# Inner tiles of six feed-forward stages in parts of 8, 8 and 6 instead of 8, 6 and 8, and where small work stands at their end

## The chip, the cores and the metric

The program runs on one core of one Trainium2 chip. The metric is device time: microseconds of the one core from start to end of a launch. The kernel before took 3107.2 us, the median of 3 runs (3106.8 to 3108.93).

## The reference

Input is x, 512 tokens of 1024 features, in float32. Twelve stages follow each other, each a residual around a normalized input. Two layers of the first block are: feed-forward, a mixer, feed-forward. Two layers of the second block are: a mixer (in layer 0 with rotary positions, in layer 1 a linear recurrence with decays), cross-attention to a memory, feed-forward. So six of the stages are feed-forward, and all six have the same form (cut to it):

```
D_MODEL = 1024; SEQ = 512; D_FF = 2816; D_FF_2 = -(-8 * D_MODEL // (3 * 256)) * 256   # = 2816

def _swiglu(x, w_gate, w_up, w_down):
    return (jax.nn.silu(x @ w_gate) * (x @ w_up)) @ w_down

x = x + MACARON * _swiglu(_rmsnorm(x, ffn1_norm), ffn1_w_gate, ffn1_w_up, ffn1_w_down)   # first block, MACARON = 0.5
x = x + swiglu(rms_norm(x, ffn_norm[layer]), ffn_w_gate_up[layer], ffn_w_down[layer])    # second block

def rope_tables(positions):          # needed by the first mixer of the second block
    inv_freq = ROPE_BASE ** (-jnp.arange(0, QK_ROPE_DIM, 2, dtype=jnp.float32) / QK_ROPE_DIM)
    ang = positions.astype(jnp.float32)[..., None] * inv_freq
    return jnp.cos(ang), jnp.sin(ang)
```

## The kernel before, in words

Everything lies with features on the 128 partitions and the 512 tokens along the row: x is 8 tiles of 128 x 512, the 2816 inner features of a feed-forward are KF = 22 inner tiles, and its output is 8 output tiles, called m = 0 to 7. The six feed-forward stages are f = 0 to 5 in the code and **FFN 0 to 5** in this text. In the list of the twelve stages (i = 0 to 11) they stand at F_STAGE = (0, 2, 3, 5, 8, 11). FFN 0 and 2 are followed by the first block's mixers, FFN 1 directly by FFN 2, FFN 3 (i = 5) by the mixer with rotary positions (M2_STAGE, i = 6), FFN 4 (i = 8) by the mixer with decays (M3_STAGE, i = 9), and FFN 5 is the end.

**Precision.** Each product is taken in three: the operands are split into a high part and a low part (high x high, high x low, low x high). Weights arrive in units of 128 x 1024 float32 in one stream, by DMAs that SP issues (line 3238) into slots; ScalarE makes the high part (`split_hi`, line 1218, tile whi), GpSimd the low part (`lo`, line 3121, wlo). Of the normalized input, ScalarE makes the high slice gxh (line 1273) and VectorE the low slice gxl (line 2161). SP loads into a slot again once the unit in it has been split.

**Parts.** The inner tiles go in three parts, `F_PARTS`: tiles 0 to 7, 8 to 13, 14 to 21. For each part the kernel computes gate and up of its tiles and then multiplies by the weights of `down`. The first two parts are taken in blocks: a product of 2 x 2 blocks is made from seven products of blocks (the steps `seven(s)`), on 256 columns, in lines 640, 641 and 644. There is a step for each inner tile (gate and up) and, for each of the first two parts, four `down` steps of two output tiles each. A product of a `down` step has 3 matmuls for each pair of inner tiles: 12 in the first part's, 9 in the second part's. The sums of blocks that the seven products need are made by VectorE (lines 2207 to 2225); some of the additions of their results are GpSimd's (`part`, line 3157), and the last ones into x are VectorE's (`c22`, line 2238, and `first_row`, line 2259; for an inner tile they go into a bank, lines 2233 and 2255). TensorE's fourth product of the next step (`fourth(s - 1)`, written for the step before it) waits for c22's result.

**The last part** is classical, on 512 columns, in lines 501 to 505: eight units, m = 0 to 7, of as many pairs of high and low inner tiles as the part has, 3 matmuls each. The first X_EARLY = 3 units are held open in three banks: first all their pairs but the last two, then the fourth product of the last inner tile, then the last two pairs of each (the "rests"). Units 3 to 7 follow whole. In FFN 5 the last unit is taken in two halves of 256 columns (`last_tile`).

**An inner tile** m passes from TensorE to VectorE's gate (line 2272), ScalarE's silu, GpSimd's scaling (`scale`, line 3129, tile f_s), VectorE's hidden product (line 2286, tile f_u), and then its high part (`hidden_hi`, ScalarE, line 1314) and its low part (`hidden_lo`, GpSimd, line 3134). These go into halves of tiles f_oddh/l, f_tur0h/l (function `hidden_tile`). Tiles of the first two parts are also turned into blocks by VectorE and ScalarE. PAIRED is the first tile of the last part.

**The residual** comes after each stage, in rounds m = 0 to 7: VectorE adds unit m's bank to x (line 2150), ScalarE makes gxh and the squares, VectorE the slice gxl (line 2161) and the sum of squares (line 2168). The next stage's first matmuls read the slices in order, the last one (m = 7) at last. When the next stage is a feed-forward, the rounds also turn the slices into blocks (`turn_parts`, `turn_lo`). The residual after FFN 3 has a second sum of squares (line 2177), and the 12 operations of `rope_angles` (lines 2021 to 2039) stand ahead of round 1 and a sign multiplication (line 2140) ahead of round 4, after ScalarE's two sines. The residual after FFN 4 has `decay_bounds` ahead of round 1, `decay_rates` ahead of 3 and `reset_positions` ahead of 4.

**Order.** Each engine's program is written out by hand in the order in which it runs; semaphores are its only waits. An instruction waits behind all that stands ahead of it on its engine. GpSimd's order at the end of an FFN is in `ffn` at line 3160 and on, VectorE's in `step(s)`.

Of the kernel before, what the change touches and what calls it, by code (L numbers as in the profile page):

```python
# [13 lines left out]
P = 128  # L14
# [43 lines left out]
F_PARTS = ((0, 8), (8, 14), (14, 22))  # L58
F_RUNS = ((0, 9), (9, 15), (15, 22))
# [116 lines left out]
def freed(u):  # L176

    if u in SEVEN:
# [9 lines left out]
          for m in range(X_EARLY + 1, KD if i == F_STAGE[5] else KD + 2)}  # L188

# [54 lines left out]
class Memory:  # L244
# [72 lines left out]
    def mixer2_tiles(self):  # L317
        outer = self.stack
        with ExitStack() as st:
# [9 lines left out]
                ("rcos", SEQ, F32), ("rsin", SEQ, F32), ("inv", 4 * 16, F32),  # L329
# [58 lines left out]
def hidden_tile(M, T, m):  # L388

    if m >= PAIRED:  # L390
        k = m - PAIRED
        name, k = ("odd", (k + 3) % 4) if k < 4 else ("tur0", k - 4)
        return seq(T[name + "h"], k), seq(T[name + "l"], k)
# [68 lines left out]
def tensor_program(pe, S, M):  # L462
# [132 lines left out]
    def last_tile(pairs):  # L595
# [4 lines left out]
        for half in range(2):  # L600
            b = next_bank("xs", 11, KD - 1, half)
            for k in range(KD):
# [5 lines left out]
            for k in range(KD):  # L608
                mm = pe.matmul(b[:, 0:HALF], seq(lo, k, P), of_half(pairs[k][0], half), start=False, stop=k == KD - 1)
# [8 lines left out]
    def ffn(f):  # L618
# [589 lines left out]
def scalar_program(act, S, M, T_in):  # L1208
    bank = M.bank

    def split_hi(u):
# [6 lines left out]
        act.activation(M.whi[r][:, :], M.raw[r][:, :], ACT.Copy).then_inc(*S.tick("hi", u))  # L1218
# [23 lines left out]
    def residual(i, keys):  # L1242
# [58 lines left out]
    def ffn(f):  # L1301
# [64 lines left out]
        def step(s):  # L1366
# [629 lines left out]
def vector_program(dve, S, M):  # L1996
# [124 lines left out]
    def residual(i, last, scale):  # L2121
# [75 lines left out]
    def ffn(f):  # L2197
# [114 lines left out]
        def step(s):  # L2312
# [781 lines left out]
def pool_program(pool, S, M):  # L3094
# [13 lines left out]
    def lo(u):  # L3108
# [6 lines left out]
        if u in SEVEN and SEVEN[u][0] == 2:  # L3115
# [5 lines left out]
        pool.tensor_tensor(M.wlo[r][:, :], M.raw[r][:, :], M.whi[r][:, :].bitcast(F32), ALU.subtract).then_inc(  # L3121
            *S.tick("lo", u))

    def ffn(f):
# [52 lines left out]
        for s, item in enumerate(SEQS[f]):  # L3177
# [19 lines left out]
            if before[0] == "tile":  # L3197
# [225 lines left out]
```

## Time and profile before

| | |
|---|---|
| median of 3 runs | 3107.2 us (3106.8 to 3108.93) |
| the profiled execution's own time | 3106.85 us |
| span of its trace | 3105.6 us |
| TensorE, matmuls (PE) | 3080.5 us busy, 99% |
| TensorE, weight loads (PEld) | 2827.1 us, 91% |
| VectorE (DVE) | 2168.9 us, 70% |
| ScalarE (ACT) | 1624.8 us, 52% |
| GpSimd (POOL) | 1650.7 us, 53% |
| matmuls | 20424 |
| DMA | 322.61 MB, mean 104 GB/s |

All is one execution, seen from its span's start, in microseconds. PE's busy time covers matmuls that overlap each other (a matmul's own duration is longer than the distance to the next one's start), so the pace of the stream is read from the starts. "x" with a number is a count of instructions. A timeline row has the start, the duration, the engine, the line of the kernel, the operation, output and inputs, and in brackets the idle time ahead of it with what ended it.

### The profile page before, as it was taken

The numbers are of one execution on the slowest core, as the hardware profiler recorded it, in microseconds if no ns is written. First come the engines' busy times: TensorE is split into PE (matmuls) and PEld (weight loads), VectorE is DVE, ScalarE is ACT, GpSimd is POOL, SyncE is SP. The second block draws the span as 40 slices with busy tenths as digits, with TensorE's granted clock in tenths as the row PEclk, the third lists the DMA queues.
The fourth block names the chain that finished last, engine by engine and source line by source line (L and its number), as shares of the span: only waits on it lengthen the run. The fifth ranks groups of instructions, "written<-read, shape, count | busy, mean of one in ns | idle before, by whom it ended". The sixth has DMA issues, their size and how long they took to land. (4 is left out here: it accounts for less than half of the span.)

```text
span 3105.6 us, 52754 instructions
## 1 busy us (share of the span) xinstructions
PE 3080.5 (99%) x20424; PEld 2827.1 (91%) x20424; DVE 2168.9 (70%) x2975; ACT 1624.8 (52%) x2567; POOL 1650.7 (53%) x994
## 2 busy tenths in 40 slices
PE   9999999999999999999999999999999999999999
PEld 8999888999989998888999877889999788889998
DVE  8776467877668774577877578558775786478773
ACT  6555433555556554335555455556554575455553
POOL 5676433677657675434767433226676112257674
PEclk9999999999999999999999999999999999999999
DMA  4323322232322232322223232322232223323232
GB/s 141 113 103 123 120 76 75 102 110 109 123 86 105 109 117 102 113 82 82 109 107 112 93 95 82 118 93 106 99 122 105 95 93 121 114 89 109 109 110 82
DMA packets 93320, 322.61 MB, mean 104 GB/s; under 512 B 10512, under 2 KB 14992, under 8 KB 93072
## 3 DMA queue, kind: packets, MB, share of 16 engines
q1 hardware_dynamic: 87680, 312.07, 28.5%
q10 hardware_dynamic: 5392, 7.17, 0.7%
q8 instruction: 164, 2.69, 0.4%
q14 instruction: 84, 0.69, 0.1%
HBM read 316.05 MB, written 2.10 MB: 102 GB/s over the span
## 5 line engine op out<-in xcount | busy, mean ns | idle before, releaser
L3121 POOL TENSOR_TENSOR wlo<-raws,whi 128x1024 fp32r<-128x1024 f32 x369 | 891.8, 2420 | 1135.8 <-ACT whi L1218 884.4
L1218 ACT ACTIVATE whi<-raws 128x1024 fp32r<-128x1024 f32 x422 | 441.0, 1051 | 159.2 <-PE bank L505 57.2
L3129 POOL TENSOR_TENSOR f_s<-f_s,R 128x512 f32<-128x512 f32 x132 | 172.4, 1306 | 193.8 <-ACT f_s L1308 192.4
L640 PE MATMUL bank<-gxh,whi 128*128 128x256 f32 x1064 | 268.8, 283 | 1.2 <-ACT acc L1364 1.2
L641 PE MATMUL bank<-gxl,whi 128*128 128x256 f32 x1064 | 268.6, 283 | 0.0
L2219 DVE TENSOR_TENSOR wlo<-banks,whi 128x1024 fp32r<-128x1024 f32 (+1 forms) x166 | 196.9, 1186 | 68.9 <-ACT whi L1335 68.9
L640 PE MATMUL bank<-f_th,f_sh 128*128 128x256 f32 x944 | 236.9, 283 | 0.0
L641 PE MATMUL bank<-f_tl,whi 128*128 128x256 f32 x944 | 236.7, 283 | 0.0
L640 PE MATMUL bank<-f_th,whi 128*128 128x256 f32 x944 | 236.7, 283 | 0.0
L641 PE MATMUL bank<-f_tl,f_sh 128*128 128x256 f32 x944 | 236.7, 283 | 0.0
L501 PE MATMUL bank<-gxh,whi 128*128 128x512 f32 x584 | 229.9, 394 | 1.4 <-DVE gxl L2161 1.4
L1335 ACT ACTIVATE whi<-banks 128x1024 fp32r<-128x1024 f32 (+1 forms) x166 | 165.2, 995 | 122.6 <-DVE banks L2212 122.2
L1364 ACT ACTIVATE sq<-bank 128x256 f32<-128x256 f32 x332 | 125.8, 379 | 194.9 <-PE bank L644 193.3
L502 PE MATMUL bank<-gxl,whi 128*128 128x512 f32 x584 | 227.4, 389 | 0.0
L3118 POOL TENSOR_TENSOR f_sl<-raws,f_sh 128x512 fp32r<-128x512 f32 x166 | 217.0, 1307 | 13.1 <-ACT f_sh L1349 13.1
L2207 DVE TENSOR_TENSOR banks<-raws 128x1024 f32<-128x1024 f32 (+1 forms) x166 | 210.0, 1265 | 0.0
L640 PEld LDWEIGHTS bank<-gxh,whi 128*128 128x128 f32 x1064 | 204.2, 192 | 1.8 <-ACT acc L1364 1.6
L641 PEld LDWEIGHTS bank<-gxl,whi 128*128 128x128 f32 x1064 | 204.2, 192 | 0.2
L2225 DVE TENSOR_TENSOR f_sl<-banks,f_sh 128x1024 fp32r<-128x1024 f32 (+1 forms) x166 | 195.3, 1176 | 0.0
L2286 DVE TENSOR_TENSOR f_u<-bank,f_s 128x512 f32<-128x512 f32 x132 | 91.3, 691 | 145.4 <-DVE f_sl L2225 83.7
L640 PEld LDWEIGHTS bank<-f_th,f_sh 128*128 128x128 f32 x944 | 181.2, 192 | 0.5 <-issue 0.2
L641 PEld LDWEIGHTS bank<-f_tl,f_sh 128*128 128x128 f32 x944 | 181.2, 192 | 0.2
(597 smaller groups left out, 9192.7 us busy)
## 6 DMA issues: line engine op xcount, KB each, us to landing
raws<-stream SPq DMA_DIRECT2D x588, 512.0 KB, 3.3
xa_mem<-memT ACTq DMA_DIRECT2D x2, 1024.0 KB, 6.2
m_dk<-decay ACTq DMA_DIRECT2D x2, 514.0 KB, 4.5
x<-xT ACTq DMA_DIRECT2D x4, 256.0 KB, 5.3
x<-xT SPq DMA_DIRECT2D x4, 256.0 KB, 6.6
outT<-x SPq DMA_DIRECT2D x2, 512.0 KB, 3.0
m_ct<-cos ACTq DMA_DIRECT2D x2, 256.0 KB, 2.6
m_sn<-sin ACTq DMA_DIRECT2D x2, 256.0 KB, 2.9
```

Source lines behind the costliest of these rows:

```text
L501: pe.matmul(out, seq(hi, k, P), h, start=first and k == 0, stop=False)
L502: pe.matmul(out, seq(hi, k, P), l, start=False, stop=False)
L640: pe.matmul(out, seq(hi, k, P), moving[k][0], start=first and k == 0, stop=False, skip_group_check=n != 1)
L641: pe.matmul(out, seq(hi, k, P), moving[k][1], start=False, stop=False, skip_group_check=n != 1)
L1218: act.activation(M.whi[r][:, :], M.raw[r][:, :], ACT.Copy).then_inc(*S.tick("hi", u))
L1335: act.activation(both(M.whi[u % SLOTS][:, :], cols), both(M.banks47[:, :], cols), ACT.Copy).then_inc(*S.tick("s13_hi", f, s))
L2207: dve.tensor_tensor(both(M.banks47[:, :], cols), both(M.raws[:, at + SEQ:at + 3 * SEQ], cols), m21[:, None, :].to_broadcast([P, 2, cols]), ...
L2219: dve.tensor_tensor(both(M.wlo[r][:, :], cols), both(M.banks47[:, :], cols), both(M.whi[r][:, :].bitcast(F32), cols), ALU.subtract).then_i ...
L2225: dve.tensor_tensor(both(T[f"sl{s % 2}"][:, SEQ:], cols), both(M.banks56[:, :], cols), both(T[f"sh{s % 2}"][:, SEQ:].bitcast(F32), cols), ...
L3118: pool.tensor_tensor(seq(T[f"sl{s % 2}"], 0), seq(M.raw[r], 1), seq(T[f"sh{s % 2}"], 0).bitcast(F32), ALU.subtract).then_inc(*S.tick("lo", u))
L3121: pool.tensor_tensor(M.wlo[r][:, :], M.raw[r][:, :], M.whi[r][:, :].bitcast(F32), ALU.subtract).then_inc(*S.tick("lo", u))
L3129: pool.tensor_tensor(T["s"][:, :], T["s"][:, :], M.R[:, :], ALU.mult).then_inc(*S.tick("silu_scaled", f, m))
```

## The change

It sets `F_PARTS` to tiles 0 to 7, 8 to 15 and 16 to 21. The second part has eight tiles, so that its `down` steps have four pairs instead of three, and the last part has six. Its units carry 768 columns of weights instead of 1024 (`unit_cols`), in the DMA as well as in both splits. The first tile of the last part (16) gets its high and low parts one step later, in the step of tile 17. `rope_angles` goes from the residual after FFN 3 to the step of its last inner tile, ahead of VectorE's `first_row`, with the DMA of the positions issued by ScalarE in that step; `decay_bounds` goes in the same way into FFN 4's last step. GpSimd makes the low part of tile 21 ahead of the split of the fourth output unit (m = 3).

```diff
-F_PARTS = ((0, 8), (8, 14), (14, 22))
-F_RUNS = ((0, 9), (9, 15), (15, 22))
+F_PARTS = ((0, 8), (8, 16), (16, 22))
+F_RUNS = ((0, 9), (9, 17), (17, 22))
...
+LAST = {U["down", f, 2, m] for f in range(6) for m in range(KD)}
+def unit_cols(u):
+    return (F_PARTS[2][1] - F_PARTS[2][0]) * P if u in LAST else UNIT
...
 # hidden_tile
-        name, k = ("odd", (k + 3) % 4) if k < 4 else ("tur0", k - 4)
+        name, k = ("odd", k) if k < 4 else ("tur0", k - 4)
...
 # TensorE, ffn
-            part(("down", f, 2, m), banks[m][:, :], pairs, range(0, 6), True, False, arrive if m == 0 else None)
+            part(("down", f, 2, m), banks[m][:, :], pairs, range(0, len(ks) - 1), True, False, arrive if m == 0 else None)
             if m == 0:
                 fourth(len(SEQS[f]) - 1)
         for m in range(X_EARLY):
-            part(("down", f, 2, m), banks[m][:, :], pairs, range(6, KD), False, True, arrive if m == 0 else None)
+            part(("down", f, 2, m), banks[m][:, :], pairs, range(len(ks) - 1, len(ks)), False, True, arrive if m == 0 else None)
...
 # ScalarE, split_hi
-        act.activation(M.whi[r][:, :], M.raw[r][:, :], ACT.Copy).then_inc(*S.tick("hi", u))
+        cols = unit_cols(u)
+        act.activation(M.whi[r][:, 0:cols], M.raw[r][:, 0:cols], ACT.Copy).then_inc(*S.tick("hi", u))
...
 # ScalarE, residual
-        if i == M2_STAGE - 1:
-            act.wait_ge(*S.at("hidden", 3, KF - 1))
-            act.dma_start(M.m2["rsin"][:, :].bitcast(I32), T_in["pos"]).then_inc(*S.tick("pos2", by=16))
...
 # ScalarE, step of an FFN
+            if after is None and i == M2_STAGE - 1:
+                act.wait_ge(*S.at("seven", f, s - 1, 4))
+                act.dma_start(M.m2["rsin"][:, :].bitcast(I32), T_in["pos"]).then_inc(*S.tick("pos2", by=16))
...
-            if before[0] == "tile":
+            if before[0] == "tile" and before[1] != PAIRED:
                 hidden_hi(before[1])
...
+            if SEQS[f][s] == ("tile", PAIRED + 1):
+                act.wait_ge(*S.at("seven", f, s - 1, 3))
+                hidden_hi(PAIRED)
...
 # VectorE, residual
-            if i == M2_STAGE - 1 and m == 1:
-                rope_angles()
-            if i == M3_STAGE - 1 and m == 1:
-                decay_bounds()
...
 # VectorE, step(s)
+            if not after and i == M2_STAGE - 1:
+                rope_angles()
+            if not after and i == M3_STAGE - 1:
+                dve.wait_ge(*S.at("seven", f, s - 1, 4))
+                decay_bounds()
             first_row(s)
...
 # GpSimd, step
-            if before[0] == "tile":
+            if item == ("tile", PAIRED + 1):
+                hidden_lo(PAIRED)
+            if before[0] == "tile" and before[1] != PAIRED:
                 hidden_lo(before[1])
...
         lo(U["down", f, 2, 2])
         scale(KF - 1)
+        hidden_lo(KF - 1)
         lo(U["down", f, 2, 3])
-        hidden_lo(KF - 1)
```

In the diff GpSimd's split and SP's DMA are cut to `unit_cols` as ScalarE's is. Memory for the mixer of stage 6 gets one more row of 512 below `rcos` ("below_rcos"), so that its two tables lie where the last step of FFN 3 no longer reads, and the weights of the last part are laid out as six rows of tiles with two of zeros behind them.

What stands in a row on VectorE at the end of FFN 3, before. L2286 is the hidden product of tile 20, L2255 and L2233 the additions of tile 21's step into its banks (`first_row` and `c22`), L2272 and the second L2286 tile 21's gate and hidden product, L2150 the residual's first round:

```order
L2286 TENSOR_TENSOR f_u<-bank,f_s 128x512
L2255 TENSOR_TENSOR bank<-bank,sq 128x512
L2233 TENSOR_TENSOR bank<-bank,acc 128x256
L2272 SCALAR_TENSOR_TENSOR bank<-bank,R 128x512
L2286 TENSOR_TENSOR f_u<-bank,f_s 128x512
L2125 MEMSET acc 128x512
L2128 MEMSET R 128x512
L2150 SCALAR_TENSOR_TENSOR x<-bank,x 128x512
L2161 SCALAR_TENSOR_TENSOR gxl<-x,lcol,gxh 128x512
L2168 TENSOR_TENSOR acc<-acc,banks 128x512
L2177 TENSOR_TENSOR R<-R,xsd 128x512
L2021 CAST m_rcos<-m_rsin 128x512
```

And in the changed kernel, right behind the hidden product of tile 20 (now line 2295): L2034 to L2052 are `rope_angles`, L2264 and L2242 the additions of tile 21's step, and tile 21's gate (now line 2281) comes next:

```order
L2034 CAST m_rcos<-m_rsin 128x512
L2036 TENSOR_SCALAR m_rcos<-m_rcos,rcol 128x512
L2038 TENSOR_SCALAR xsd<-m_rcos 128x512
L2040 TENSOR_SCALAR xsd<-xsd 128x512
L2043 SCALAR_TENSOR_TENSOR m_rcos<-xsd,m_rcos 128x512 x3
L2045 TENSOR_SCALAR m_rsin<-m_rcos 128x512
L2046 TENSOR_SCALAR m_rcos<-m_rcos 128x512
L2048 TENSOR_SCALAR xsd<-m_rcos 128x512
L2050 TENSOR_TENSOR m_rcos<-m_rcos,xsd 128x512
L2052 TENSOR_SCALAR m_rcos<-m_rcos 128x512
L2264 TENSOR_TENSOR bank<-bank,sq 128x512
L2242 TENSOR_TENSOR bank<-bank,acc 128x256
```

The twelve operations moved from behind the residual's first round to between tile 20's hidden product and tile 21's additions.

What stands in a row on GpSimd at the end of FFN 0, before. L3121 is the split of a weight unit, L3129 the scaling and L3134 the low part of an inner tile (20, then 21):

```order
L3121 TENSOR_TENSOR wlo<-raws,whi 128x1024 x2
L3129 TENSOR_TENSOR f_s<-f_s,R 128x512
L3134 TENSOR_TENSOR f_tur0l<-f_u,f_tur0h 128x512
L3121 TENSOR_TENSOR wlo<-raws,whi 128x1024
L3129 TENSOR_TENSOR f_s<-f_s,R 128x512
L3121 TENSOR_TENSOR wlo<-raws,whi 128x1024
L3134 TENSOR_TENSOR f_tur0l<-f_u,f_tur0h 128x512
L3121 TENSOR_TENSOR wlo<-raws,whi 128x1024 x42
```

And in the changed kernel, where L3136, L3144 and L3149 are the same three:

```order
L3136 TENSOR_TENSOR wlo<-raws,whi 128x768 x2
L3144 TENSOR_TENSOR f_s<-f_s,R 128x512
L3149 TENSOR_TENSOR f_tur0l<-f_u,f_tur0h 128x512
L3136 TENSOR_TENSOR wlo<-raws,whi 128x768
L3144 TENSOR_TENSOR f_s<-f_s,R 128x512
L3149 TENSOR_TENSOR f_tur0l<-f_u,f_tur0h 128x512
L3136 TENSOR_TENSOR wlo<-raws,whi 128x768 x5
L3136 TENSOR_TENSOR wlo<-raws,whi 128x1024 x38
```

The low part of tile 21 moved ahead of the fourth unit's split, and the eight splits of the last part are 768 wide.

## Rows read from the trace of the kernel before

**Rows 1.** The page's busy time by engine.
```profile
PE 3080.5 (99%) x20424; PEld 2827.1 (91%) x20424; DVE 2168.9 (70%) x2975; ACT 1624.8 (52%) x2567; POOL 1650.7 (53%) x994
```

**Rows 2.** Waits of PE by line and releaser: us in total, times, longest us.
```profile
PE bank L640 <- DVE x L2238: 6.1, 6, 1.1
```

**Rows 3.** Timeline of PE, its longest wait, after FFN 3.
```profile
1768.00 0.77 PE L501 MATMUL bank<-f_oddh,whi 128*128 128x512 f32 x1 [5.30 <-ACT whi L1218]
```

**Rows 4.** Windows: stretch, us, busy (count) by engine, PEclk, DMA share, GB/s.
```profile
1768.00:1773.00 5.00, 5.00 (x12) 3.94 (x13) 3.87 (x5) 3.60 (x7) 3.65 (x2) 0.50 0.31 103
```

**Rows 5.** Timeline of PE, blocks of FFN 0: start us, us, engine, line.
```profile
228.67 0.28 PE L640 MATMUL bank<-f_oddh,f_sh 128*128 128x256 f32 x1
...
229.75 0.28 PE L640 MATMUL bank<-f_tur0h,whi 128*128 128x256 f32 x1
```

**Rows 6.** Timeline of PE, whole units of FFN 0's last part.
```profile
326.39 0.39 PE L501 MATMUL bank<-f_oddh,whi 128*128 128x512 f32 x1
...
331.83 0.39 PE L501 MATMUL bank<-f_oddh,whi 128*128 128x512 f32 x1
```

**Rows 7.** Timeline of PE, a wait in FFN 0, in brackets.
```profile
217.80 0.35 PE L640 MATMUL bank<-f_tur0h,f_sh 128*128 128x256 f32 x1 [1.01 <-DVE x L2238]
```

**Rows 8.** One tile: ns min/median/max, first, last start us; forms.
```profile
L1328 ACT ACTIVATE f_tur0h<-xsd x24: 845/847/849, 45.8 to 2928.5; 128x768 fp32r<-128x768 f32 x24
...
L3149 POOL TENSOR_TENSOR f_tur0l<-xsd,f_tur0h x24: 1850/1857/1872, 46.8 to 2932.0; 128x768 fp32r<-128x768 f32 x24
```

**Rows 9.** Timeline of DVE and ACT, residual of FFN 0.
```profile
323.87 0.69 DVE L2150 SCALAR_TENSOR_TENSOR x<-bank,x 128x512 f32<-128x512 f32 x1 [5.52 <-PE bank L490]
...
328.67 1.04 ACT L1218 ACTIVATE whi<-raws 128x1024 fp32r<-128x1024 f32 x1
```

**Rows 10.** Timeline of DVE and POOL beside each other, residual of FFN 3.
```profile
1775.88 2.44 POOL L3121 TENSOR_TENSOR wlo<-raws,whi 128x1024 fp32r<-128x1024 f32 x1 [1.56 <-ACT whi L1218]
...
1775.99 2.62 DVE L2140 TENSOR_SCALAR m_rsin<-m_rsin,rcol 128x512 f32<-128x512 f32 x1
```

**Rows 11.** Timeline of DVE, residual of FFN 1: first two rounds, last slice.
```profile
869.51 0.69 DVE L2150 SCALAR_TENSOR_TENSOR x<-bank,x 128x512 f32<-128x512 f32 x1 [5.52 <-PE bank L490]
...
872.43 0.69 DVE L2150 SCALAR_TENSOR_TENSOR x<-bank,x 128x512 f32<-128x512 f32 x1
...
900.91 0.93 DVE L2161 SCALAR_TENSOR_TENSOR gxl<-x,lcol,gxh 128x512 fp32r<-128x512 f32 x1 [0.79 <-ACT gxh L1273]
```

**Rows 12.** Timeline of DVE and PE, residual of FFN 4 and what follows.
```profile
2409.51 0.69 DVE L2150 SCALAR_TENSOR_TENSOR x<-bank,x 128x512 f32<-128x512 f32 x1 [5.52 <-PE bank L490]
...
2425.81 0.69 DVE L2150 SCALAR_TENSOR_TENSOR x<-bank,x 128x512 f32<-128x512 f32 x1
...
2444.06 0.50 PE L516 MATMUL bank<-gxh,whi 128*128 128x512 f32 x1 [0.70 <-DVE gxl L2161]
```

**Rows 13.** Lines of DVE, residual of FFN 3: busy us, mean ns, idle before.
```profile
L2177 DVE TENSOR_TENSOR R<-R,xsd 128x512 f32<-128x512 f32 x8 | 5.5, 682 | 0.0
```

**Rows 14.** Timeline of DVE, first and last of the 12 angle operations.
```profile
1757.94 0.42 DVE L2021 CAST m_rcos<-m_rsin 128x512 f32<-128x512 int32 x1
...
1764.00 0.43 DVE L2039 TENSOR_SCALAR m_rcos<-m_rcos 128x512 f32<-128x512 f32 x1
```

**Rows 15.** Timeline of DVE, the addition to x in `down`, FFN 1.
```profile
663.62 0.41 DVE L2238 SCALAR_TENSOR_TENSOR x<-bank,x 128x256 f32<-128x256 f32 x1
```

**Rows 16.** Timeline of all engines, last inner tile's step of FFN 3.
```profile
1736.72 0.69 DVE L2286 TENSOR_TENSOR f_u<-bank,f_s 128x512 f32<-128x512 f32 x1 [2.29 <-POOL f_s L3129]
...
1738.06 0.70 DVE L2255 TENSOR_TENSOR bank<-bank,sq 128x512 f32<-128x512 f32 x1 [0.64 <-PE bank L644]
...
1738.16 1.30 POOL L3134 TENSOR_TENSOR f_tur0l<-f_u,f_tur0h 128x512 fp32r<-128x512 f32 x1 [1.52 <-ACT f_tur0h L1314]
...
1740.69 2.39 POOL L3121 TENSOR_TENSOR wlo<-raws,whi 128x1024 fp32r<-128x1024 f32 x1 [1.24 <-ACT whi L1218]
...
1743.40 0.28 PE L640 MATMUL bank<-f_th,f_sh 128*128 128x256 f32 x1
```

More of the change, by code:

```diff
@@ L328, in mixer2_tiles @@
                 ("pr0", 10 * P, F32), ("pr1", 10 * P, F32), ("pt0", 10 * P, F32), ("pt1_end", 2 * P, F32), ("ub0", SEQ + 16, F32), ("ub1", SEQ + 16, F32),
-                ("rcos", SEQ, F32), ("rsin", SEQ, F32), ("inv", 4 * 16, F32),
+                ("below_rcos", SEQ, F32), ("rcos", SEQ, F32), ("rsin", SEQ, F32), ("inv", 4 * 16, F32),
                 ("mx0", NB, F32), ("mx1", NB, F32), ("sums0", NB, F32), ("sums1", NB, F32), ("first", 16, F32)])
@@ L601, in last_tile @@
             b = next_bank("xs", 11, KD - 1, half)
-            for k in range(KD):
+            for k in range(len(pairs)):
                 for t in pairs[k]:
@@ L607, in last_tile @@
             pe.wait_ge(*S.at(*low_part(u)))
-            for k in range(KD):
-                mm = pe.matmul(b[:, 0:HALF], seq(lo, k, P), of_half(pairs[k][0], half), start=False, stop=k == KD - 1)
+            for k in range(len(pairs)):
+                mm = pe.matmul(b[:, 0:HALF], seq(lo, k, P), of_half(pairs[k][0], half), start=False,
+                               stop=k == len(pairs) - 1)
             mm.then_inc(*S.tick("last_half", half))
@@ L3120, in lo @@
             return
-        pool.tensor_tensor(M.wlo[r][:, :], M.raw[r][:, :], M.whi[r][:, :].bitcast(F32), ALU.subtract).then_inc(
-            *S.tick("lo", u))
+        cols = unit_cols(u)
+        pool.tensor_tensor(M.wlo[r][:, 0:cols], M.raw[r][:, 0:cols], M.whi[r][:, 0:cols].bitcast(F32),
+                           ALU.subtract).then_inc(*S.tick("lo", u))
     def ffn(f):
@@ L3237, in sync_program @@
                 sp.wait_ge(*S.at("s13" if row == 2 else "s4", f, s))
-        sp.dma_start(M.raw[r][:, :], T_in["stream"][u]).then_inc(*S.tick(f"loaded{r}", u, by=16))
+        cols = unit_cols(u)
+        sp.dma_start(M.raw[r][:, 0:cols], T_in["stream"][u][:, 0:cols]).then_inc(*S.tick(f"loaded{r}", u, by=16))
         if u == U[("m2", 7)]:
@@ L3281, in tail_units @@
         if c == 2:
-            out.append(m_tiles(tiles[ks].reshape(UNIT, -1)))
+            rows = np.zeros((KD, *tiles.shape[1:]), w.dtype)
+            rows[0:b - a] = tiles[ks]
+            out.append(m_tiles(rows.reshape(UNIT, -1)))
             continue
```

## The prediction

> **What bounds the kernel now.** I read the page's busy shares first, then the list of waits, then the timelines where a wait stood. TensorE is busy 99% of the span [rows 1]: the time is a stream of matmuls plus a few waits, and an edit counts by what it does to the stream and by the waits it makes or ends. The largest wait, on VectorE's line 2238, comes six times, 1.0 us each [rows 2]: once in each of the six feed-forward stages (FFN 0 to 5). The other large one is a single wait of 5.30 us at the end of FFN 3, in which TensorE's granted clock falls: the next 5 us run at 0.50, the 1.2 GHz level [rows 3, 4].
>
> So four things are to be priced: the stream, the six waits, the angles' new place, and, since the eight last output units of an FFN become shorter, who keeps up with them.
>
> **The stream.** In the blocked part nine 256-column matmuls start in 229.75 - 228.67 = 1.08 us, 0.120 us each [rows 5]. A plain unit of 24 matmuls of 512 columns takes 331.83 - 326.39 = 5.44 us, 0.227 us each [rows 6]. The second inner part goes from six tiles to eight: 4 pairs of outputs x 7 products x 3 matmuls more = 84 x 0.120 = +10.08 us. The last part goes from eight to six: 8 units x 2 tiles x 3 = 48 x 0.227 = -10.88 us (FFN 5, whose last unit is in halves of 12 x 0.120, -10.96). That is -0.80 us a stage, **-4.9 us** in six.
>
> The Trainium skill (TensorE: Matmul & The Clock Gate, "Back-to-back issue gap") gives an isolated gap of columns / 2.4 + 2.5 ns, 109 and 216 ns here. An estimate by it is 84 x 0.109 - 48 x 0.216 = -1.2 us a stage, -7.2 in all. The trace does not agree for 256 columns (0.120), and the narrow matmuls are those that are added.
>
> **The six waits.** They fall in the second block of `down` steps, where VectorE's addition to x is late and TensorE's fourth product waits for it, 1.01 us [rows 7]. A step there is 7 x 9 matmuls = 7.56 us; the first block, with 7 x 12 = 10.08 us and the same work beside it, has no such wait: the list counts six in all [rows 2]. With eight tiles the second block is the first one's equal. Each wait costs 1.01 plus 0.16, since the matmul before it shows 0.28 but would have been followed after 0.12 [rows 5]. 6 x 1.17 = **-7.1 us**. The bound the other way: they all stay, 0. I take the first block as the nearest case.
>
> **Who keeps up in the tail.** I count from T0, the first residual addition to x. The first of the three banks held open is ready 0.2 us before T0. Before, two more rests (2 x 1.36), five units (5 x 5.44) and 14 matmuls of the next stage (3.17) stand between it and the moment TensorE asks for the last slice of the normalized input: T0 + 32.9. After: 2 x 0.68 + 5 x 4.08 + 3.17 - 0.2 = T0 + 24.7. The eight rounds of VectorE and ScalarE that make these slices get nothing shorter but the weight splits: 0.85 us on ScalarE and 1.86 on GpSimd at 768 columns [rows 8], where 1024 took 1.04 [rows 9] and about 2.4 [rows 10].
>
> - FFN 0 and 2. A round takes 872.43 - 869.51 = 2.92 us [rows 11], under 4.08, so it catches up. But ScalarE splits the fifth unit's weights only after two rounds: it started at T0 + 4.80 (328.67) [rows 9], now ends at 5.65, and TensorE wants it at 5.24. +0.5 each, **+1.1 us**.
> - FFN 1. Here the rounds also turn the blocks of the next FFN, and the last slice was done at 901.84, T0 + 32.3 [rows 11], beside TensorE's T0 + 32.9. That chain hardly waited for TensorE. I take 1.2 us off it, for GpSimd operations that hold a slice up and become 0.55 shorter: T0 + 31.2 against 24.7, **+6.5 us**. From both sides: nothing comes off, +7.7; three such operations and a half more, +5.
> - FFN 4. The fourth addition starts at 2425.81, T0 + 16.3, behind the row of small decay operations, and TensorE asked for the last slice at 2444.06, T0 + 34.5, having waited 0.70 [rows 12]. It was 1.6 over its due time already. Shorter splits take some 2 us off, so T0 + 32.6, 7.9 over the new due time: **+6.3 us** net.
> - FFN 3. A round has a second sum of 0.68 [rows 13]: 3.6 us, seven rounds 25.2, the last slice 2.2 more, ScalarE's two sines about 1.2, the sign multiplication and its blocking by GpSimd (it took 2.62 us beside an operation of 2.44 [rows 10]) about 2, further blocking 0.5. T0 + 31.3, **+6.6 us**, between +5 and +8.
> - FFN 5 has no slices to make, so its rounds are shorter still. Its last half loses part of its gain where the row of reciprocals comes from ScalarE: **+0.2 us**.
>
> **The angles.** Their removal from the second round ends the wait of 5.30 and the 12 slow matmuls after it. With 5.30 + 12 x 0.2 = 7.7 and the start of the first slow matmul, 0.2, that is **-7.9 us**. They were 12 operations from 1757.94 to 1764.43, 6.49 us [rows 14], GpSimd having nothing beside them. Now they stand in VectorE's queue behind the product that ends at 1737.41, and what is queued behind them is the last tile's two additions, 0.70 (1738.06) and 0.41 us [rows 15, 16]. The second frees TensorE's fourth product. That started at 1743.40 and is due three matmuls earlier, at 1742.7 [rows 16]. If nothing else holds VectorE: 1737.4 + 6.5 + 1.1 + 0.1 = 1745.1, a stall of 2.4. But GpSimd has two operations in that stretch, 1.30 us at 1738.16 and the split at 1740.69, now 1.86 [rows 16], and in [rows 10] an operation of VectorE from SBUF to SBUF ended 0.3 us after GpSimd's, 2.62 us for what takes 0.43. Blocked by both, it is 2.4 + 3.2 - 0.2 = 5.4 us. I take 5.4, by that row, and add 2.4 for the clock, since a wait of 5.30 did cost it: 12 matmuls at 0.42 or a little more (5.00 us for 12) instead of 0.227 [rows 3, 4]. **+7.8 us**; the bounds are +2.4 and +7.8. The positions' DMA, issued now behind the step's fourth product, must land before 1737.4, which I take it to do; each microsecond later is one more.
>
> On this place the Trainium skill (SBUF — State Buffer, "Who interferes with whom") has a rule against the change: VectorE in a two-port mode, or with two SBUF inputs against a GpSimd read, and GpSimd lock each other out for a whole instruction. The trace agrees [rows 10]. By the rule both GpSimd operations are paid in full, without it neither.
>
> Moved ahead of the fourth unit's split, GpSimd's low part of tile 21 now ends about 5.7 us after the fourth product, and TensorE wants it 6.8 after, having only five of six tiles of three units to do first (15 x 0.227 x 2). It waits for nothing; without the move it would end at 7.0 and cost 0.2 in each stage. Tile 16's halves, put one tile later, wait for a product long done.
>
> **Sum.** -4.9 - 7.1 + 1.1 + 6.5 + 6.3 + 6.6 + 0.2 - 7.9 + 7.8 = **+8.6 us** on the profiled execution's 3106.85: 3115.5. The median of before is 3107.2, 0.3 above that execution, so the forecast is 0.27% slower.
>
> **Rivals.**
> - *The angles run beside GpSimd* (chance 0.25), the case on the other side. Their stall is 2.4, too short for the clock: 5.4 us less, +3.2, 3110. Not slower than a measurement can tell. For it: no row shows these very operations against GpSimd. Against it: [rows 10]. [...]
> - *The clock falls in the new tail waits too* (0.15). FFN 1, 3 and 4 would each have three to four idle microseconds before the last slice, split by a few matmuls, where 5.3 sufficed once. Two falls at 2.4: 3120.
> - *The six waits stay* (0.08), since GpSimd's queue in the second block has the low part of tile 15 too: +7.1, 3122.5.
> - *The tails are hidden* (0.07): the rounds of FFN 1, 3 and 4 shorten with their units, so 19 us of waits vanish: 3096. Against it: in FFN 1 the rounds took as long as TensorE's 5.44 a unit with only 0.56 us to spare at the end [rows 11].
>
> **How the numbers follow.** The forecast has 0.40, 0.05 is left for what I don't see. What a measurement here can tell from no change is about 0.2%, 6.2 us: 3101 to 3113.4. Faster is the last rival, 0.07. Within are most of the first (0.21) and the low quarter of the forecast (0.09): 0.30. Slower is the rest, 0.63. The range reaches from the low side of the first rival, with each tail 2 us shorter, to the second and third with a little more: 3103 to 3123.
>
> **What would show it.** In the profile after: no wait on the `down` addition in the second block; 12 angle operations before the last tile's additions in FFN 3, one or two over 1.5 us, and a wait of TensorE there of 2 to 6 us; at the start of the stages behind FFN 1, 3 and 4 waits for a slice (gxl) of 3 us or more. If those starts show none, the prediction is wrong and the kernel faster.

## The result and the profile after

The changed kernel took 3115.52 us, the median of 9 runs (3115.15 to 3117.3), against 3107.03 (3106.72 to 3108.93) before: ratio 1.0028, 95% interval 1.0019 to 1.0037. The profiled execution took 3115.32 us. The forecast was 3115.5, from 3103 to 3123.

The page's busy times of the changed kernel, which answer to [rows 1]:

```profile
PE 3084.5 (99%) x20634; PEld 2837.9 (91%) x20634; DVE 2204.4 (71%) x2999; ACT 1629.1 (52%) x2579; POOL 1635.4 (53%) x1006
```

The largest waits of TensorE in it (engine, line, released by: us in total, times, longest us):

```profile
PE bank L509 <- ACT whi L1228: 7.8, 7, 3.6
PE bank L509 <- DVE gxl L2170: 5.2, 4, 2.7
PE bank L649 <- DVE bank L2242: 4.4, 1, 4.4
PE bank L524 <- DVE gxl L2170: 2.1, 1, 2.1
```

The six waits of [rows 2] and the one of 5.30 [rows 3] are gone. In their place stand one wait for the last inner tile's addition (L2242, in FFN 3's last step) and a dozen in the tails, for the high part of a unit's weights (whi) or for a low slice (gxl). The timeline of TensorE has the larger ones; the first is one of the small ones of FFN 0, the next two are FFN 1's, then three of FFN 3 and one of FFN 4:

```profile
335.66 0.47 PE L509 MATMUL bank<-f_oddh,whi 128*128 128x512 f32 x1 [0.37 <-ACT whi L1228]
...
901.81 0.50 PE L509 MATMUL bank<-gxh,whi 128*128 128x512 f32 x1 [1.05 <-DVE gxl L2170]
905.27 0.79 PE L509 MATMUL bank<-gxh,whi 128*128 128x512 f32 x1 [2.73 <-DVE gxl L2170]
...
1760.44 0.36 PE L649 MATMUL bank<-f_th,f_sh 128*128 128x256 f32 x1 [4.35 <-DVE bank L2242]
...
1778.32 0.47 PE L509 MATMUL bank<-f_oddh,whi 128*128 128x512 f32 x1 [1.70 <-ACT whi L1228]
...
1800.23 0.50 PE L524 MATMUL bank<-gxh,whi 128*128 128x512 f32 x1 [2.13 <-DVE gxl L2170]
...
2438.47 0.77 PE L509 MATMUL bank<-f_oddh,whi 128*128 128x512 f32 x1 [3.61 <-ACT whi L1228]
```

A matmul that shows 0.79 or 0.77 runs at the lower clock. The windows behind these waits show it (stretch: us, then busy time and count by engine, the granted clock, the DMA share, GB/s):

```profile
905.27:911.83 6.56, 6.56 (x16) 5.16 (x17) 4.89 (x9) 3.41 (x5) 4.71 (x2) 0.53 0.59 187
1760.44:1764.79 4.35, 4.35 (x18) 3.87 (x19) 0.70 (x1) 1.33 (x2) 0.71 (x1) 0.61 0.01 4
1778.32:1783.00 4.68, 4.68 (x21) 3.85 (x22) 3.33 (x5) 3.64 (x7) 2.89 (x2) 1.00 0.30 112
...
2438.47:2444.00 5.53, 5.53 (x13) 4.42 (x14) 4.61 (x6) 1.99 (x3) 2.55 (x2) 0.50 0.28 95
```

After 2.73 us behind one of 1.05, after 4.35 and after 3.61 the clock is 0.53, 0.61 and 0.50 over the next 4 to 6 us, so at the 1.2 GHz level for most or all of them; after 1.70 it stays at 1.00.

### The profile page after: what moved, and what is told of

The parts are those of the page before. It is cut to its first block and busy times, and to the rows that moved or that the text cites. A ratio compares the mean times of both kernels' runs of the same rounds, so it can differ in the third digit from the quotient of the medians.

```text
span 3114.1 us, 53252 instructions
## 1 busy us (share of the span) xinstructions
PE 3084.5 (99%) x20634; PEld 2837.9 (91%) x20634; DVE 2204.4 (71%) x2999; ACT 1629.1 (52%) x2579; POOL 1635.4 (53%) x1006
## 5 line engine op out<-in xcount | busy, mean ns | idle before, releaser
L3136 POOL TENSOR_TENSOR wlo<-raws,whi 128x1024 fp32r<-128x1024 f32 (+1 forms) x369 | 865.1, 2348 | 1106.1 <-ACT whi L1228 844.2
L1228 ACT ACTIVATE whi<-raws 128x1024 fp32r<-128x1024 f32 (+1 forms) x422 | 431.1, 1028 | 151.2 <-PE bank L513 57.2
L3144 POOL TENSOR_TENSOR f_s<-f_s,R 128x512 f32<-128x512 f32 x132 | 172.4, 1306 | 203.2 <-ACT f_s L1315 201.4
L2228 DVE TENSOR_TENSOR wlo<-banks,whi 128x1024 fp32r<-128x1024 f32 x166 | 203.3, 1225 | 80.9 <-ACT whi L1342 80.9
L1342 ACT ACTIVATE whi<-banks 128x1024 fp32r<-128x1024 f32 x166 | 170.2, 1026 | 122.6 <-DVE banks L2221 122.6
L2216 DVE TENSOR_TENSOR banks<-raws 128x1024 f32<-128x1024 f32 x166 | 217.3, 1309 | 0.0
L2234 DVE TENSOR_TENSOR f_sl<-banks,f_sh 128x1024 fp32r<-128x1024 f32 x166 | 201.7, 1215 | 0.0
```

The source lines that it names most:

```text
L1228: act.activation(M.whi[r][:, 0:cols], M.raw[r][:, 0:cols], ACT.Copy).then_inc(*S.tick("hi", u))
L1342: act.activation(both(M.whi[u % SLOTS][:, :], cols), both(M.banks47[:, :], cols), ACT.Copy).then_inc(*S.tick("s13_hi", f, s))
L2216: dve.tensor_tensor(both(M.banks47[:, :], cols), both(M.raws[:, at + SEQ:at + 3 * SEQ], cols), m21[:, None, :].to_broadcast([P, 2, cols]), ...
L2228: dve.tensor_tensor(both(M.wlo[r][:, :], cols), both(M.banks47[:, :], cols), both(M.whi[r][:, :].bitcast(F32), cols), ALU.subtract).then_i ...
L2234: dve.tensor_tensor(both(T[f"sl{s % 2}"][:, SEQ:], cols), both(M.banks56[:, :], cols), both(T[f"sh{s % 2}"][:, SEQ:].bitcast(F32), cols), ...
L3136: pool.tensor_tensor(M.wlo[r][:, 0:cols], M.raw[r][:, 0:cols], M.whi[r][:, 0:cols].bitcast(F32), ALU.subtract).then_inc(*S.tick("lo", u))
```

## The terms of the sum, beside what they measured

I added up, stage by stage, by how much each matmul started later than 0.120 us (behind one of 256 columns) or 0.227 us (behind one of 512) after the one before it, in both traces. "Slow matmuls" are those at the lower clock behind a wait: what they took beyond those paces. The terms in us:

| term | forecast | measured |
|---|---|---|
| stream | -4.9 | -4.9, by count and pace, not measured by itself |
| six waits | -7.1 | -7.1 |
| FFN 0 and 2, fifth unit's weights | +1.1 | +1.1 |
| FFN 1, tail | +6.5 | +9.2 (6.0 of waits, 3.2 of slow matmuls) |
| FFN 3, angles out of the residual | -7.9 | -7.9 |
| FFN 3, angles in the step | +7.8 | +6.2 (4.5 and 1.7 of slow matmuls) |
| FFN 3, tail | +6.6 | +4.2 |
| FFN 4, tail | +6.3 | +5.7 (of which 2.5 slow matmuls) |
| FFN 5 | +0.2 | +1.7 |
| sum | +8.6 | +8.2; the end of TensorE's work moved by 8.5 |

So the total is closer than its parts: FFN 1 and 5 cost 4.2 more than forecast, FFN 3 and 4 4.6 less. That they cancel to 0.4 is luck. The rest, 0.3, I did not place.

## The experiments

Each ran against the kernel before on the same chip; "ratio" is to it, with its 95% interval. To compare stages I use a mark: by how many microseconds VectorE's last addition to x in a stage's residual (round 7) starts later than in the kernel before. The waits for the last slices come behind that addition, so what an FFN's tail costs is in the mark of the stage behind it. In the changed kernel the mark was -1.50 at FFN 0, 3.02 at FFN 1, 4.60 at FFN 2, 5.02 in the stage behind FFN 3, 8.62 in the one behind FFN 4. What a stage gives or costs is the difference of two marks.

**1. The parts alone.**

The cut shows it against the changed kernel.

```diff
 F_PARTS = ((0, 8), (8, 16), (16, 22))      # stays, with 768-column units
 # rope_angles and decay_bounds back in the residual ahead of round 1
-        hidden_lo(KF - 1)
         lo(U["down", f, 2, 3])
+        hidden_lo(KF - 1)
```

> The new parts (8, 8, 6) with the 768-column units, and everything else where it stood before: the angles and the decay bounds in the residual, GpSimd's low part of tile 21 behind the fourth unit's split. My theory (the chain of rounds on VectorE and ScalarE sets the end of FFN 1, 3 and 4): the changed kernel's terms stay in FFN 0, 1, 2 and 5 (-1.3, +7.5, -1.4, about 0), FFN 4 about +4; in FFN 3 the 6.5 us of angles in round 1 lengthen a chain that has 8 us less of TensorE's work over it, so its wait grows from 5.3 to about 14 us: FFN 3 about +6.5 against before. Sum about +15: 3122, between 3119 and 3125, so the angles' move is worth about 6 us to the changed kernel. Rival (the angles' place is worth nothing once the parts are changed, since their stall in the step is as long): the time of the changed kernel, 3115.5.

Measured: 3115.39 us, ratio 1.0026 (1.0015 to 1.0036), the changed kernel's own time. My expectation (3122) failed, the rival held. TensorE's timeline at the end of FFN 3:

```profile
1778.13 0.76 PE L514 MATMUL bank<-f_oddh,whi 128*128 128x512 f32 x1 [7.81 <-ACT whi L1234]
```

The wait grew from 5.30 to 7.81 and not to 14, and the mark behind FFN 3 was 4.85, where the changed kernel has 5.02. From FFN 2's mark to that one both kernels lose 0.4 us: moving the angles into the step took away this wait and put as much in its place. The other two moves (decay bounds, GpSimd's order) show no gain beyond 0.4 us in any mark. The six waits are gone here too, so the parts alone end them.

**2. The angles alone**, parts 8, 6, 8.

```diff
-            if i == M2_STAGE - 1 and m == 1:
-                rope_angles()
 # VectorE, last step of FFN 3, with the positions' DMA in ScalarE's same step
+            if not after and i == M2_STAGE - 1:
+                rope_angles()
             first_row(s)
```

> The kernel before with only the 12 angle operations (and the positions' DMA) moved into the last inner tile's step of FFN 3, parts 8, 6, 8. My theory: the wait of 5.30 us and its slow matmuls go (-7.9), a stall of 4.4 to 5 us with 1 us of slow clock comes in the step, and the tail has room: -2 to -2.5 us, 3104.5 to 3105.2; two of the operations are blocked by GpSimd for 1 to 2 us each. Rival (they run beside GpSimd, stall 2.4): -5.5, 3101.5. Rival (the step's stall delays everything behind it as much as the residual did): 3107.

Measured: 3107.66 us, ratio 1.0001 (0.9992 to 1.0009): no gain, the last rival (by the marks FFN 3 gave 0.6 us). The timeline of VectorE, then of GpSimd, then of TensorE:

```profile
1738.66 1.08 DVE L2043 CAST m_rcos<-m_rsin 128x512 f32<-128x512 int32 x1 [1.24 <-DMA m_rsin<-pos]
...
1740.76 2.61 DVE L2049 TENSOR_SCALAR xsd<-xsd 128x512 f32<-128x512 f32 x1
```

```profile
1740.70 2.39 POOL L3151 TENSOR_TENSOR wlo<-raws,whi 128x1024 fp32r<-128x1024 f32 x1 [1.24 <-ACT whi L1234]
```

```profile
1749.08 0.55 PE L654 MATMUL bank<-f_th,f_sh 128*128 128x256 f32 x1 [5.51 <-DVE bank L2257]
```

The stall was 5.5 instead of 4.4: the positions came 1.24 us too late for the first operation, which then took 1.08 instead of 0.42 beside GpSimd's low part, and the fourth, 0.43 us long when alone, took 2.61 beside GpSimd's split and ended 0.28 after it. In the changed kernel's profile the positions were there in time; in that of experiment 9, with the same step, they came 1.09 late.

**3. The angles in the gap ahead of the residual.**

```diff
 # the changed kernel; rope_angles not in the last step, but
+        if i == M2_STAGE - 1:
+            rope_angles()                  # ahead of the residual's memset and round 0
```

> The changed kernel with the 12 angle operations moved once more: behind the hidden product of tile 21, ahead of the residual's first round, where VectorE was idle for about 5 us. My theory: the stall of 4.4 us and the slow matmuls behind it go (-5.5); 6.5 us of work, with one or two GpSimd operations that block it, in a gap of 5.1 makes the first round 1.4 to 4.5 us late, and the tail of FFN 3 waits that much longer, since its chain sets the end: 3111.4 to 3114.5, about 3113. Rival (the tail of FFN 3 is not set by that chain but by TensorE or the weights): the full 5.5, 3110.

Measured: 3114.57 us, ratio 1.0022 (1.0013 to 1.0031), at the upper end of what I expected (3114.5). VectorE's and GpSimd's timelines there:

```profile
1760.66 1.43 DVE L2047 TENSOR_SCALAR xsd<-m_rcos 128x512 f32<-128x512 f32 x1
1762.13 1.95 DVE L2049 TENSOR_SCALAR xsd<-xsd 128x512 f32<-128x512 f32 x1
```

```profile
1760.52 1.29 POOL L3164 TENSOR_TENSOR f_tur0l<-f_u,f_tur0h 128x512 fp32r<-128x512 f32 x1 [1.53 <-ACT f_tur0h L1330]
1761.77 2.02 POOL L3151 TENSOR_TENSOR wlo<-raws,whi 128x768 fp32r<-128x768 f32 x1
```

Both GpSimd operations of the gap were paid, 1.0 and 1.5 us; the first round came about 6 us later, counted from FFN 2's mark, than in experiment 1, and TensorE waited 7.87 us at 1777.07 for the weights of the fifth unit, which ScalarE splits behind round 1. From FFN 2's mark to the one behind FFN 3 this kernel loses 0.45 us and the changed one 0.42: the gap gave FFN 3 nothing over the step. The 1 us in the time is FFN 1's, whose slow matmuls cost less in this profile.

**4. Parts 8, 8, 6 in FFN 0 and 2 only**, angles in the gap.

```diff
+EIGHT = (0, 2)
+F_PARTS = [((0, 8), (8, 16), (16, 22)) if f in EIGHT else ((0, 8), (8, 14), (14, 22)) for f in range(6)]
```

> Parts 8, 8, 6 in FFN 0 and 2 only (where the stage behind is a mixer with slack), 8, 6, 8 in the others, decay bounds in the residual, and the angles in the gap ahead of FFN 3's first round. My theory adds up by stage: FFN 0 and 2 -1.3 and -1.4; FFN 3 -7.9 and 1 to 3 back for a first round that is late by 1 to 3.5 us with 1.6 us of slack: 3097 to 3100, about 3098.3. Rival (what a stage costs depends on the stages before it, as by DMA or clock): anything else, 3101 or more.

Measured: 3100.79 us, ratio 0.9982 (0.9973 to 0.9991), faster than before, but above the 3097 to 3100 that I expected. By the marks FFN 0 gave 1.35, FFN 2 1.3 and FFN 3 3.2; the last was expected at 5 to 7, and a wait of 3.2 us for the fifth unit's weights stands there. FFN 0 and 2 gave what I expected of them without the others' change; the angles were still in a bad place. Of the six waits the four in the stages with 8, 6, 8 are left:

```profile
PE bank L654 <- DVE x L2262: 4.0, 4, 1.0
```

**5. GpSimd's low part of tile 14 later.**

```diff
-            if before[0] == "tile":
+            if item == ("tile", PAIRED + 1):
+                hidden_lo(PAIRED)
+            if before[0] == "tile" and before[1] != PAIRED:
                 hidden_lo(before[1])
```

> The kernel before (parts 8, 6, 8) with one move: GpSimd's low part of tile 14, the first of the last part, goes from the step of the second block's first pair of outputs to the step of tile 15. My theory of the six waits after the changed kernel: in the second block GpSimd's queue (splits, scaling and this low part of 1.3 us) makes its additions late, so that VectorE's addition and TensorE's fourth product are late by 1.0; with 1.3 us taken out of that queue all six waits go: -5.5 to -7, 3100 to 3101.5. Rival (a step of 7.56 us is too short for GpSimd's work whatever stands in it, so only the parts of eight tiles cure it): the waits stay, 3106.8, or come one step later.

Measured: 3106.8 us, ratio 1.0001 (0.9992 to 1.0009). The waits stayed, all six (6.1 us in total). GpSimd's and VectorE's timelines at the first show why:

```profile
215.21 1.30 POOL L3201 TENSOR_TENSOR x<-x,sq 128x512 f32<-128x512 f32 x1
```

```profile
216.61 0.69 DVE L2290 SCALAR_TENSOR_TENSOR x<-bank,x 128x512 f32<-128x512 f32 x1 [1.27 <-POOL x L3201]
217.22 0.41 DVE L2269 SCALAR_TENSOR_TENSOR x<-bank,x 128x256 f32<-128x256 f32 x1
```

The low part stood behind GpSimd's additions in its queue, so it could not have made them late. TensorE waits for the second of VectorE's additions, which needs nothing of GpSimd's last one but stands behind the first, which does.

**6. That small addition first.**

```diff
+            if SEQS[f][s] == ("down", 1, 0):
+                c22(s)
             first_row(s)
```

> The kernel before with one move on VectorE: in the step of the second block's first pair of outputs, the small addition to x (line 2238) goes ahead of the large one (line 2259). The trace of before shows the small one's last input from GpSimd at 215.27 and its product of TensorE done before that, but in the queue it stood behind the large one, which waited for GpSimd until 216.53. My theory now (the wait is VectorE's order behind a late GpSimd, not the step's length): the addition is done at about 215.8 and all six waits of 1.0 us go: -6 to -7, 3100 to 3101. Rival (the step of 7.56 us is too short for GpSimd's work, so that the wait moves to the next thing that GpSimd makes): less than 2 us.

Measured: 3106.47 us, ratio 1.0000 (0.9991 to 1.0009). TensorE's waits:

```profile
PE bank L658 <- ACT sq L1384: 2.9, 6, 0.5
PE bank L658 <- DVE x L2268: 1.8, 6, 0.6
```

The addition was done at 215.65 and the wait at 217.8 is gone, but half of it comes back 3.6 us later, for ScalarE (0.46 us at 221.45), and 0.2 to 0.6 at the next steps. By the marks FFN 0 gains 0.2 us, FFN 3 0.6 and the others 0.13 or less; the time does not show it. So the six waits are better read as a chain through GpSimd, VectorE and ScalarE that takes longer than a step of 7.56 us: a step of 10.08 ends them (experiments 1 and 4), and neither of the two other orders that I tried does.

**7. The angles in two pieces, changed kernel, and 8. the same with parts 8, 6, 8.**

```diff
         c22(len(SEQS[f]) - 1)
+        rope_angles(0, 8)                  # only in FFN 3
         gate(KF - 1)
+        rope_angles(8, 12)
         hidden(KF - 1)
```

> The changed kernel with the 12 angle operations in two pieces: the first eight behind tile 21's last addition and ahead of its gate, where VectorE waited for TensorE, the last four between gate and hidden product, where it waited for GpSimd. My theory: nothing waits for VectorE there, GpSimd has at most one split beside them, so the stall of 4.4 us and its slow matmuls go and the tail's waits stay: -5 to -6 against the changed kernel, 3110. Rival (as in the two runs that had the angles in the residual or in the gap ahead of it, the tail grows by what the stall gives): 3114.5 to 3115.5.

> The kernel before (parts 8, 6, 8) with the angles alone moved, in the same two pieces. My theory: the wait of 5.30 us and the 12 slow matmuls go and nothing comes for them: -7.9, 3099. Bounds: if GpSimd's split blocks one operation and the gate comes 1 to 2 us late, 3101. Rival (a wait of that size returns in the tail, since the rounds of FFN 3 set its end in any case): 3103 or more.

Measured: 3108.95 us, ratio 1.0007 (0.9999 to 1.0016), and 3101.25, ratio 0.9981 (0.9973 to 0.9990). In the first the stall of 4.35 us and its slow matmuls are gone and the tail's waits stayed at 1.69 and 2.1: 6.5 us by the time, of which the marks put 4.9 in FFN 3, since a wait of 1.07 for tile 21's low part comes in. The second is a little above the 3101 of my bound; FFN 3 gave 6.4 by the marks, and the same wait is 1.19. VectorE's timeline ahead of it has three blocked operations:

```profile
1740.58 2.56 DVE L2051 TENSOR_SCALAR xsd<-m_rcos 128x512 f32<-128x512 f32 x1
...
1747.67 1.73 DVE L2064 TENSOR_TENSOR m_rcos<-m_rcos,xsd 128x512 f32<-128x512 f32 x1
1749.43 2.51 DVE L2066 TENSOR_SCALAR m_rcos<-m_rcos 128x512 f32<-128x512 f32 x1
```

**9. A shorter chain in FFN 1's tail.**

```diff
+        if f == 2:                          # the blocks that FFN 1's residual turns
+            out, x11, x21, x22, b12 = (64 columns of each instead of 256)
```

This kernel leaves out three quarters of those blocks' columns and serves only to time the chain.

> The changed kernel with VectorE's four turning operations of each pair of slices in FFN 1's residual on 64 columns instead of 256, so part of the blocks of FFN 2's input is not computed. Twelve of them stand ahead of the last slice and shorten from about 0.48 to 0.2 us. My theory (the chain of rounds from the first addition to the last slice sets the end of FFN 1): the last slice comes 3 to 4 us earlier, the waits of 6.0 us there shrink to 2 to 3, and the slow matmuls behind them (about 3 us) go at least in part: 3109 to 3112. Rival (the weights or TensorE's own units set it): the waits stay, 3115.5.

Measured: 3111.63 us, 3.9 less than the changed kernel, ratio 1.0014 (1.0006 to 1.0023). The four operations fell from 0.48 to 0.28 us and the mark at FFN 1's end from 3.02 to 0.61: 12 x 0.2 = 2.4 us, all of which TensorE got; the first of its two waits there, 1.05, is gone. The second is 2.70 still, and the slow matmuls behind it cost 1.9 instead of 3.2. At FFN 2's mark 3.7 us are gained. The profiled execution, 3113.41 us, was slower than the median: in it FFN 3 lost 2 us more than in the changed kernel's profile, with the positions late. The chain of VectorE's rounds sets the end of FFN 1.

**10. The kernel before with the moves of 6 and the angles in pieces of 5, 4 and 3, and 11. with parts 8, 8, 6 in FFN 0 and 2 and earlier splits.**

```diff
+        rope_angles(0, 5)
         gate(KF - 1)
+        rope_angles(5, 9)
         hidden(KF - 1)
+        rope_angles(9, 12)
 # 11 alone, ScalarE: one round earlier
-        residual(i, [None, None] + [("down", f, 2, m) for m in range(2, KD)])
+        residual(i, [None] + [("down", f, 2, m) for m in range(2, KD)] + [None])
```

> The kernel before (8, 6, 8) with that move and with the 12 angle operations in three pieces around tile 21's gate and hidden product (5, 4 and 3). If both gains are real and independent: -6.5 for the six waits, -5.6 (the two pieces alone) to -7.9 for the angles: 3092.5 to 3095. Rival (the place of the pieces does not matter, GpSimd blocks two or three of them anywhere): 3095.

> The same, with parts 8, 8, 6 in FFN 0 and 2 only, and ScalarE's splits of the last units one round earlier in every FFN's residual. FFN 0 and 2 give their -0.8 us of stream each and, if the earlier splits take away the 0.37 us wait for the fifth unit's weights (0.53 with its start), nothing back: -1.6 against the kernel with the parts as before: 3091 to 3093.5. The earlier split may also end the small wait for weights in FFN 4 (0.36). Rival (ScalarE's split ahead of a slice delays the rounds where their chain sets the end, in FFN 1, 3 and 4): 0 to +2 against it.

Measured: 3100.27 us, ratio 0.9978 (0.9969 to 0.9987), and 3103.07, ratio 0.9989 (0.9980 to 0.9998). The first fell short of its 3095 because the six waits gave nothing; by the marks FFN 3 gave 7.3 us, of which 0.6 had come with the addition alone (experiment 6). The second is slower than the first where I expected it faster: by the marks FFN 0, 2 and 4 gave 1.8, 2.0 and 1.4 us more, and FFN 3 cost 8.9 more. There VectorE's second sum, 0.68 us in [rows 13], stood beside GpSimd's split in six rounds. VectorE's timeline in one of them, then GpSimd's, then TensorE's wait:

```profile
1762.65 2.57 DVE L2207 TENSOR_TENSOR R<-R,xsd 128x512 f32<-128x512 f32 x1
```

```profile
1762.28 2.39 POOL L3172 TENSOR_TENSOR wlo<-raws,whi 128x1024 fp32r<-128x1024 f32 x1 [3.13 <-DVE gxl L2191]
```

```profile
1789.89 0.80 PE L533 MATMUL bank<-gxh,whi 128*128 128x512 f32 x1 [4.75 <-DVE gxl L2191]
```

**12. The same without the earlier splits.**

> Parts 8, 8, 6 in FFN 0 and 2 only, the angles in three pieces (5, 4 and 3 operations), the small addition first in the four FFNs of 8, 6, 8, and ScalarE's splits where they were. Against the kernel with the parts as before (3100.3) FFN 0 and 2 should give -1.3 and -1.4 us each, as they did in the changed kernel and in the first mixed one: 3097 to 3098.5. Rival (the gain of the two stages comes back elsewhere, as it did in the mixed kernel with the earlier splits, whose FFN 3 waited 6 us for its last two slices): 3100 or more; if FFN 3 shows no wait for those slices here, the earlier splits were the cause there.

Measured: 3096.81 us, ratio 0.9965 (0.9953 to 0.9978): the lowest median of all, some 11 us under the kernel before and 19 under the changed one; its interval overlaps that of experiment 10. The marks give 1.53 for FFN 0, 1.3 for FFN 2 and 7.7 for FFN 3, and the waits of FFN 3 for slices are gone. That is the earlier splits' fault shown: nothing else differs between 11 and 12. In FFN 0, 2 and 4 they had gained 0.5, 0.7 and 1.5 us; keeping them there alone was not tried.

## Why the prediction was right, and where not

**The six waits.** All went, as forecast, and by the longer step; the nearest case (the first block) was the right one. (6 x 1.17 is 7.0, not 7.1; the six measured 7.1.) GpSimd's queue, my reason for the rival, held only in part: experiments 5 and 6 change the place of one item each, and the chain through GpSimd, VectorE and ScalarE stays longer than the step.

**The tails.** The count from T0 was right: TensorE's work over the rounds became 8 us shorter and the rounds did not, so the ends of FFN 1, 3 and 4 went over to the chain of VectorE and ScalarE; experiment 9 shows that for FFN 1, for the other two it is read from the trace. In FFN 1 the forecast had the last slice at T0 + 31.2. VectorE's timeline, T0 and the last slice:

```profile
874.11 0.69 DVE L2159 SCALAR_TENSOR_TENSOR x<-bank,x 128x512 f32<-128x512 f32 x1 [3.48 <-PE bank L498]
...
903.92 1.29 DVE L2170 SCALAR_TENSOR_TENSOR gxl<-x,lcol,gxh 128x512 fp32r<-128x512 f32 x1 [0.79 <-ACT gxh L1280]
```

905.21 - 874.11 = 31.1. What the sum left out is the clock: the rival "the clock falls in the new tail waits too", to which I gave 0.15, came true in FFN 1 and FFN 4, 3.2 and 2.5 us. The time is not its 3120 only because other terms were too large. In FFN 4 TensorE waited not for the last slice but for a weight unit, at 2438.47: ScalarE's split stands in its queue behind a high slice, and that behind VectorE's row of decay operations. ScalarE's timeline:

```profile
2436.36 0.72 ACT L1280 ACTIVATE gxh<-x,rcol 128x512 fp32r<-128x512 f32 x1 [6.68 <-DVE x L2159]
...
2437.50 0.83 ACT L1228 ACTIVATE whi<-raws 128x768 fp32r<-128x768 f32 x1
```

The step that failed for FFN 3 is the estimate of its rounds. The sines, the sign multiplication and further blocking were put at 3.7 us over seven rounds of 3.6, of which 2 for the multiplication, by [rows 10]. It took 0.48, since no split stood beside it. VectorE's timeline, first round, multiplication, last slice:

```profile
1771.22 0.69 DVE L2159 SCALAR_TENSOR_TENSOR x<-bank,x 128x512 f32<-128x512 f32 x1 [2.37 <-PE bank L498]
...
1785.49 0.48 DVE L2149 TENSOR_SCALAR m_rsin<-m_rsin,rcol 128x512 f32<-128x512 f32 x1
...
1799.09 1.09 DVE L2170 SCALAR_TENSOR_TENSOR gxl<-x,lcol,gxh 128x512 fp32r<-128x512 f32 x1 [0.79 <-ACT gxh L1280]
```

The last slice was done at T0 + 29.0, not T0 + 31.3 (the terms in the forecast add up to 31.1), and the tail came to 4.2 instead of 6.6.

The sign that I named, waits of 3 us or more for a slice behind FFN 1, 3 and 4, came only in FFN 1, in two pieces (1.05 and 2.73). FFN 3 had 2.13 for a slice and 1.70 for weights, FFN 4 its 3.61 for weights.

**The angles.** The stall is 4.35, under the 5.4 forecast and over the rival's 2.4. VectorE's and GpSimd's timelines:

```profile
1750.34 0.42 DVE L2034 CAST m_rcos<-m_rsin 128x512 f32<-128x512 int32 x1
...
1751.32 1.43 DVE L2038 TENSOR_SCALAR xsd<-m_rcos 128x512 f32<-128x512 f32 x1
...
1753.24 3.67 DVE L2043 SCALAR_TENSOR_TENSOR m_rcos<-xsd,m_rcos 128x512 f32<-128x512 f32 x3
```

```profile
1751.16 1.30 POOL L3149 TENSOR_TENSOR f_tur0l<-f_u,f_tur0h 128x512 fp32r<-128x512 f32 x1 [1.52 <-ACT f_tur0h L1321]
...
1753.69 1.95 POOL L3136 TENSOR_TENSOR wlo<-raws,whi 128x768 fp32r<-128x768 f32 x1 [1.23 <-ACT whi L1228]
```

Both GpSimd operations block, as assumed, but each only for what is left of it when VectorE's next operation comes: 1.0 and 1.5 us (3.67 for three that take 2.15), where I had counted 3.2 in full. And I had treated the move as +7.8 against -7.9 without asking what the angles cost if they stayed. Experiment 1 answers: the same. So for this kernel the move is neutral, and so it is alone (experiment 2); in experiments 7 and 8, where VectorE would else have waited for others, it gains 6.5 and 5.6 us by the time. The rival with the stall of 2.4 called that too short for the clock. No run had such a stall: after waits of 2.13 and less the clock stayed, after one of 2.70 (experiment 9) it fell.

**FFN 5.** Forecast +0.2, measured +1.7: its last half waits 0.25 for the reciprocals, and slow matmuls at the very end cost 1 more. How much of it is the change's stays open: from the last round to TensorE's last matmul the kernels with FFN 5 left as before lost 0.4 to 1.9 us against the one profile of before, with no edit there.

## What to carry to other kernels

Where blocks trade work between a stage's middle and its tail, count the tail from the first moment that the other engines' chain can start, and compare TensorE's work over that chain before and after; here 8 us less cover turned a chain that was nearly free into 19 us of waits and slow matmuls. The choice may differ from stage to stage: 8, 8, 6 paid where the chain is short (FFN 0 and 2) and not in FFN 1, 3 and 4; FFN 5 by itself was not tried. A row of small operations should go where its engine waits for others and nobody waits for it, in pieces if the gaps are short.

## What the runs showed of the hardware

VectorE operations from SBUF to SBUF that alone take 0.43 or 0.68 us took up to 2.6 beside a GpSimd operation and ended after it: tensor_scalar, with a single input, by 0.28 to 0.29 us, tensor_tensor, with two, by 0.55 (experiment 11). The Trainium skill (SBUF — State Buffer, "Who interferes with whom") says as much of modes that use both ports and of two SBUF inputs; experiment 11 shows the price when a schedule lines the two up round after round, 1.9 us each time. A chain of equal rounds can fall into that step or out of it by a change elsewhere: between experiments 11 and 12 only ScalarE's splits were moved.

The clock fell after waits of 3.2 (experiment 4, granted 0.68 over the next 5 us), 3.6, 4.4, 5.3 and 5.5 us, and also after 2.73 us that followed one of 1.05 and after 2.70 without such a one ahead (experiment 9, granted 0.67 over the next 5.1 us); after 2.13 and 1.70 it did not. After the wait of 2.73 the same kernel text cost 3.2 us of slow matmuls in one profile and 2.0 in another (experiment 3, whose FFN 1 is the changed kernel's, granted 0.74 over the next 6.5 us where the changed kernel had 0.53).
